# A seven-product form for five instead of four of the eight pairs of k-tiles in the gate and up products of a fused decoder kernel

## The chip, the cores and the metric

The kernel runs on one core of a Trainium2 chip. Time is the device time of the whole program in microseconds (us), the median of several runs. One more execution was profiled; its trace gives every instruction a start, a duration and, where its engine stood idle before it, the instruction that ended the idle time. Engines are called as in the profile: PE (TensorE, the matmuls), PEld (its weight loads), DVE (VectorE), ACT (ScalarE), POOL (GpSimd), SP (SyncE, which issues the loads).

## The reference, cut to what matters

The program is two residual blocks over 256 tokens of width 2048 in float32. The change touches only the last sublayer, the gated feed-forward layer with a hidden width of 5632:

```python
hf = rms_norm_2(x, g_ffn[layer])
x = x + (jax.nn.silu(hf @ w_gate[layer]) * (hf @ w_up[layer])) @ w_down[layer]
return rms_norm_2(x, g_final)
```

## The kernel before

**Split operands.** Each float32 operand is kept as a high part (a copy in the fp32r type, `hi`, `xh`, `wsh`) and a low part (the operand minus its high part, `lo`, `xl`, `wsl`). A product is three matmuls: high by high, high by low, low by high. For weights ACT makes the high part and DVE the low part, from a landed block `raw`. A block is 512 rows by 512 columns (1 MB); the copies work on halves of it (128 x 1024 elements), and `hi` and `lo` hold four halves each (HS = LS = 4), so ACT and DVE can be at most four halves ahead of PE. There are four `raw` blocks; SP loads a block again once DVE has made the last low part of the block that was in it.

**The feed-forward layer** runs in turns `i` of 512 hidden columns. Turns 0 and 1 are plain. In turns 2 to 10 (`ffn_turn`, nine of them) gate and up are computed together: step `v` (0 to 7) takes the pair of k-tiles 2v and 2v+1, and `raw` then holds four 128 x 512 parts, gate k0, gate k1 (half 0), up k0, up k1 (half 1), called w[0] to w[3] in the code. Two token halves times two k-tiles times gate and up are eight 128x128 by 128x512 products, 24 matmuls: a plain step (`plain_unit`). For the steps in the tuple `BILINEAR` it is a Strassen-Winograd scheme of seven products, 21 matmuls (`bilinear_unit`), on four sums of weight parts (`wsums`) and four of token parts (`sh`, `sl`, made once during turn 1 by `tokens_made`, `tokens_high`, `tokens_low`). The four weight sums are w0+w2, w2+w3, w0+w2+w3 and that plus w1. DVE makes them, ACT their high parts (`wsh`), DVE their low parts (`wsl`). Plain steps use differences of tokens, kept in `ah`/`al` and, for more than four plain steps, in `dh`/`dl`.

After step 7 follow four down-projection blocks of the turn before (units of 24 matmuls in `unit`). During them DVE adds up the seven products (`partial_sums`, `gate_sums`) and adds the down products to the residual X (`accumulate`, four a turn; the last, with c = 3, comes in step 1 of the next turn, where `hidden` and `hidden_blocks` also finish the hidden values of the turn before). Those go through DRAM and back, rearranged, into `fT` (POOL's queue), and `hidden_high` (ACT) and `hidden_low` (DVE) split them for the down blocks.

**Order.** Every engine runs its list in program order; nothing is reordered between engines but by semaphores. The wait of one instruction therefore holds back all that stands behind it on that engine. In a bilinear step DVE's list before is: two of the sums in one instruction (L2079, 1024 elements), low part of half 0, third sum (L2086), low parts of two sums (L2070), fourth sum (L2098), low part of w[3] alone (512 elements); the low parts of the other two sums stand in the next, plain step. ACT takes half 0, half 1 (only w[3], 512 elements), the first two sums (L1194), and the last two sums behind half 0 of the next step. The sums of the next turn's step 0 are made at the end of the down blocks (`start_next`). `gfb`, the gain row of the last norm (1 MB), is loaded in turn 0.

Of the kernel before, what the change touches and what calls it, by code (L numbers as in the profile page):

```python
# [52 lines left out]
BILINEAR = (0, 2, 4, 6)  # L53
# [72 lines left out]
def build(nc, x, ret_w_in, ret_w_out, pool_w_in, pool_w_grp, pool_b_grp, pool_w_out, final_norm, mem, positions,  # L126
# [3 lines left out]
    with ExitStack() as ctx:  # L130
# [6 lines left out]
        def stage(*tensors):  # L137
# [25 lines left out]
            ("sh", [P, len(BILINEAR), 4, P], F32R), ("sl", [P, len(BILINEAR), 4, P], F32R),  # L163
            ("dh", [P, max(0, KV - len(BILINEAR) - 4) + 1, SEQ], F32R), ("dl", [P, max(0, KV - len(BILINEAR) - 4) + 1, SEQ], F32R))
# [13 lines left out]
        junk = sb("junk", [P, NB])  # L178
        krT = sb("krT", [P, 2, SEQ])
        qrp = sb("qrp", [P, 2, TT, P])  # L180
# [46 lines left out]
        def as_blocks(tile):  # L227
# [44 lines left out]
        sg, fg, gfb, fblk, fT, wsums, wsh, wsl, p1s, u2 = stage(  # L272
            ("sg", [P, TT, NB]), ("fg", [P, TT, NB]), ("gfb", [P, D]),
            ("fblk", [P, TT, 4, 4 * BK]), ("fT", [P, TT * 4, 4 * BK]),
            ("wsums", [P, 4, NB]), ("wsh", [P, 4, NB], F32R), ("wsl", [P, 4, NB], F32R),
            ("p1s", [P, NB]), ("u2", [P, NB]))
        u3 = junk
# [39 lines left out]
        sums13_made, sum2_made, sum4_made = sem("sums13_made"), sem("sum2_made"), sem("sum4_made")  # L317
# [90 lines left out]
        def four(U):  # L408

            return raw[:, U % RAW].rearrange("p a b n -> p (a b) n")  # L410

# [57 lines left out]
        def _(sp):  # L469
# [166 lines left out]
            for u in range(4):  # L636
                load(Pos(FU + 2 * u), rows(w_gate[0], 512 * u, 0))
                load(Pos(FU + 2 * u + 1), rows(w_up[0], 512 * u, 0))
                if u == 1:
                    sp.wait_ge(half_used, 2 * FU)  # L640
                    sp.dma_start(gfb[:, :], g_final.rearrange("(a n) -> a n", a=1).broadcast_to([P, D])).then_inc(gf_in, 16)
# [10 lines left out]
            for j in range(4):  # L652
                load(Pos(DOWN_U + j), rows(w_down[0], (FC - 1) * NB, NB * j))
            out_v = out[0].rearrange("(t p) d -> p t d", p=P)
# [52 lines left out]
        def _(act):  # L707
# [441 lines left out]
            def tokens_high(v):  # L1149

                act.wait_ge(tok_made, v + 1)
                if v in BILINEAR:
                    dst, srcs = sh[:, BILINEAR.index(v)], x_sums
# [20 lines left out]
            def pair_high(U, i, v, h):  # L1174
# [6 lines left out]
                k = slice(1, 2) if h and v in BILINEAR else slice(0, 2)  # L1181
                act.activation(hi[:, (U.at * 2 + h) % HS, k, :], raw[:, U % RAW, h, k, :], ACT.Copy).then_inc(hi_ready, 1)  # L1182

            def high_sums(i, v, part):

                n = sums_at(i, v)
                if part == 0:
                    act.wait_ge(sums13_made, n + 1)
                else:
                    act.wait_ge(sum4_made, n + 1)  # L1190
                if n:
                    act.wait_ge(sums_used, 2 * n - 1 + part)
                at = slice(2 * part, 2 * part + 2)
                act.activation(wsh[:, at, :], wsums[:, at, :], ACT.Copy).then_inc(sums_high, 1)  # L1194
# [77 lines left out]
        def _(dve):  # L1272
# [708 lines left out]
            def tokens_made(v):  # L1981

                ks = slice(2 * v, 2 * v + 2)
# [10 lines left out]
            def tokens_low(v):  # L1994

                dve.wait_ge(tok_high, v + 1)
                if v in BILINEAR:
                    n = BILINEAR.index(v)
                    dst, high, srcs = sl[:, n], sh[:, n], x_sums
# [834 lines left out]
```

## Time and profile before

| | |
|---|---|
| median of 3 runs | 2486.75 us (2486.75 to 2487.12) |
| the profiled execution: its own time | 2486.79 us |
| its span, first to last instruction | 2485.0 us |
| PE busy, 10962 matmuls | 2472.1 us (99%) |
| DVE busy | 1771.4 us (71%) |
| ACT busy | 1276.0 us (51%) |
| granted TensorE clock, mean | 0.999 of full speed |

The profiled execution took 2486.79 us, 1.8 us more than its span, and agrees with the median of the timed runs. How to read it: durations of neighbouring instructions on one engine overlap in the trace by a little, so what an instruction costs in a row of others is the distance between starts. "Idle before" names the time in which the engine stood still and who ended it.

### The profile page before, as it was taken

What the parts mean: (1) busy time and instruction counts of PE and PEld (TensorE: products, weight loads), DVE (VectorE), ACT (ScalarE), POOL (GpSimd) and SP (SyncE); (2) the same over time, 40 slices, a digit from 0 to 9 for tenths busy, and PEclk for the clock granted to TensorE, in tenths of its full rate; (3) what the DMA queues carried; (4) which work ended last, traced back from release to release, by engine and by line L of the source; (5) the groups of instructions that cost most, each with busy time, mean ns of one, the idle gap of its engine ahead of it and who ended that gap; (6) DMA issues with size and microseconds to landing.
All of it is one profiled execution on the core that took longest, in us unless ns stands there. A gap on an engine that the chain in (4) does not pass through costs nothing.

```text
span 2485.0 us, 28892 instructions
## 1 busy us (share of the span) xinstructions
PE 2472.1 (99%) x10962; PEld 2036.7 (82%) x10962; DVE 1771.4 (71%) x2253; ACT 1276.0 (51%) x1619; POOL 192.0 (8%) x319
## 2 busy tenths in 40 slices
PE   9999999999999999999999999999999999999998
PEld 7888788888888888888888889888888888888887
DVE  6665665665675666675666866776678899988897
ACT  6454444444555444444545556566555555555554
POOL 0010000000011000010001100010100000000000
PEclk9999999999999999999999999999999999999999
DMA  9667666666688777776778754667766666666664
GB/s 333 208 223 221 208 212 211 204 218 202 210 241 259 231 233 223 226 234 210 228 238 262 235 180 149 233 203 220 229 211 220 220 217 212 210 211 218 218 210 148
DMA packets 263610, 545.31 MB, mean 219 GB/s; under 512 B 14768, under 2 KB 21040, under 8 KB 263088
## 3 DMA queue, kind: packets, MB, share of 16 engines
q1 hardware_dynamic: 242304, 477.39, 59.3%
q0 software_dynamic: 21168, 66.08, 9.5%
q8 instruction: 87, 1.43, 0.2%
q14 instruction: 51, 0.42, 0.1%
HBM read 508.29 MB, written 35.13 MB: 219 GB/s over the span
## 4 chain that ended last, share of the span: by engine, by line
PE 92%; DVE 5%; issue 2%; ACT 0%; DMA 0%; POOL 0%; DVEq 0%; ACTq 0%
PE job L2266 25%; PE job L2267 25%; PE job L2272 25%; DVE lo L2060 1%; PE group L2693 1%; PE group L2692 1%; PE group L2702 1%; PE att L2702 1%; PE att L2692 1%; PE att L2693 1%; PE job L2643 1%; PE job L2644 1%; PE job L2645 1%; DVE X L1343 1%; PE att L2643 1%
## 5 line engine op out<-in xcount | busy, mean ns | idle before, releaser
L1287 DVE TENSOR_TENSOR lo<-raw,hi 128x1024 fp32r<-128x1024 f32 (+1 forms) x736 | 879.2, 1213 | 504.8 <-ACT hi L729 483.9
L729 ACT ACTIVATE hi<-raw 128x1024 fp32r<-128x1024 f32 (+1 forms) x736 | 768.9, 1054 | 867.1 <-PE job L2272 808.9
L2266 PE MATMUL job<-hi,xh 128*128 128x512 f32 (+1 forms) x1696 | 663.0, 391 | 0.3 <-ACT hi L729 0.3
L2267 PE MATMUL job<-hi,xl 128*128 128x512 f32 (+1 forms) x1696 | 657.2, 388 | 0.0
L2272 PE MATMUL job<-lo,xh 128*128 128x512 f32 (+1 forms) x1696 | 451.0, 388 | 0.0
L2266 PEld LDWEIGHTS job<-hi,xh 128*128 128x128 f32 x1696 | 318.5, 188 | 68.5 <-issue 2.4
L2267 PEld LDWEIGHTS job<-hi,xl 128*128 128x128 f32 x1696 | 318.5, 188 | 66.4 <-issue 2.1
L2272 PEld LDWEIGHTS job<-lo,xh 128*128 128x128 f32 x1696 | 317.3, 188 | 65.1
L2266 PE MATMUL job<-hi,ah 128*128 128x512 f32 x832 | 325.9, 392 | 0.0
L2267 PE MATMUL job<-hi,al 128*128 128x512 f32 x832 | 323.8, 389 | 0.0
L2272 PE MATMUL job<-lo,ah 128*128 128x512 f32 x832 | 222.5, 389 | 0.0
L2266 PEld LDWEIGHTS job<-hi,ah 128*128 128x128 f32 x832 | 156.2, 188 | 32.8 <-issue 0.4
L2272 PEld LDWEIGHTS job<-lo,ah 128*128 128x128 f32 x832 | 156.2, 188 | 32.6
L2267 PEld LDWEIGHTS job<-hi,al 128*128 128x128 f32 x832 | 156.2, 188 | 32.3
L1182 ACT ACTIVATE hi<-raw 128x1024 fp32r<-128x1024 f32 (+1 forms) x144 | 133.2, 948 | 91.6 <-PE job L2272 42.8
L2060 DVE TENSOR_TENSOR lo<-raw,hi 128x1024 fp32r<-128x1024 f32 (+1 forms) x144 | 153.8, 1082 | 4.4 <-ACT hi L1182 4.4
L2266 PE MATMUL job<-hi,mh 128*128 128x512 f32 (+1 forms) x400 | 155.3, 388 | 0.2 <-ACT hi L729 0.2
L2267 PE MATMUL job<-hi,ml 128*128 128x512 f32 (+1 forms) x400 | 154.0, 385 | 0.0
L1343 DVE TENSOR_TENSOR X<-job,X 128x512 f32<-128x512 f32 x168 | 107.8, 683 | 63.2 <-PE job L2272 62.9
L1194 ACT ACTIVATE wsh<-wsums 128x1024 fp32r<-128x1024 f32 x72 | 76.1, 1057 | 75.8 <-DVE wsums L2079 59.8
L2272 PE MATMUL job<-lo,mh 128*128 128x512 f32 (+1 forms) x400 | 105.3, 385 | 0.0
L2070 DVE TENSOR_TENSOR wsl<-wsums,wsh 128x1024 fp32r<-128x1024 f32 x72 | 87.5, 1215 | 0.0
(409 smaller groups left out, 2534.5 us busy)
## 6 DMA issues: line engine op xcount, KB each, us to landing
raw<-in_ret_w_in SPq DMA_DIRECT2D x94, 1024.0 KB, 5.2
raw<-in_pool_w_in SPq DMA_DIRECT2D x64, 1024.0 KB, 5.6
raw<-in_w_down SPq DMA_DIRECT2D x44, 1024.0 KB, 5.2
raw<-in_w_gate SPq DMA_DIRECT2D x72, 512.0 KB, 3.9
raw<-in_w_up SPq DMA_DIRECT2D x72, 512.0 KB, 4.8
raw<-in_ret_w_out SPq DMA_DIRECT2D x32, 1024.0 KB, 5.3
raw<-in_pool_w_out SPq DMA_DIRECT2D x32, 1024.0 KB, 5.3
raw<-in_w_in SPq DMA_DIRECT2D x28, 1024.0 KB, 6.0
```

Source lines behind the costliest of these rows:

```text
L729: act.activation(hi[:, (U.at * 2 + h) % HS, :, 0:n], src, ACT.Copy).then_inc(hi_ready, 1)
L1182: act.activation(hi[:, (U.at * 2 + h) % HS, k, :], raw[:, U % RAW, h, k, :], ACT.Copy).then_inc(hi_ready, 1)
L1194: act.activation(wsh[:, at, :], wsums[:, at, :], ACT.Copy).then_inc(sums_high, 1)
L1287: dve.tensor_tensor(lo[:, (U.at * 2 + h) % LS, :, 0:n], src, hi[:, (U.at * 2 + h) % HS, :, 0:n].bitcast(F32), ALU.subtract).then_inc(lo_re ...
L1343: ins = dve.tensor_tensor(xs, pair[J % 2][t][:, :], xs, ALU.add)
L2060: dve.tensor_tensor(lo[:, (U.at * 2 + h) % LS, k, :], raw[:, U % RAW, h, k, :], hi[:, (U.at * 2 + h) % HS, k, :].bitcast(F32), ALU.subtrac ...
L2070: dve.tensor_tensor(wsl[:, at, :], wsums[:, at, :], wsh[:, at, :].bitcast(F32), ALU.subtract).then_inc(sums_low, 1)
L2266: pe.matmul(o, oh[:, kt, ts], w, start=first and k == 0, stop=False)
L2267: pe.matmul(o, ol[:, kt, ts], w, start=False, stop=False)
L2272: ins = pe.matmul(pair[J % 2][t][:, 0:n], oh[:, kt, ts], lo[:, H % LS, k, 0:n], start=False, stop=last and k == 1)
L2643: pe.matmul(o, oh, wh, start=start, stop=False)
L2692: pe.matmul(o[:, :], oh, hi[:, H, k], start=opens and k == 0, stop=False)
```

## The change

The tuple becomes `(0, 2, 3, 5, 6)`: step 3 and step 5 take the seven-product form and step 4 gives it up, which makes five such steps and three plain ones. With it:

- The sum w0+w2 is written in place over w[2] in `raw`; half 1 of the block then holds that sum and w[3], and is copied and subtracted as a full half. ACT's copy of half 1 waits for the sum (`sum1_made`).
- The other three sums stand in `wsums` (3 x 512) and go through ACT in one instruction and through DVE in one, of 1536 elements. `wsh` and `wsl` have two places used in turn.
- The four sums are four DVE instructions of 512 elements instead of one of 1024 and two of 512. The last two wait each for the one that it builds on.
- ACT's copy of the sums comes behind both halves of its own step and ahead of the next step's; DVE's low part of them comes at the head of the next step where that is bilinear (3 and 6), else behind the low part of its half 0 (1, 4 and 7).
- PE does four products (12 matmuls) of a bilinear step before it needs the sums, then three (9 matmuls).
- `hidden_high` and `hidden_low` move from step 6 to step 4.
- The fifth set of token sums lies over `krT` and another place, and turn 1 makes the tokens of step 6 last. The load of `gfb` moves behind the last weight load.

```diff
-BILINEAR = (0, 2, 4, 6)
+BILINEAR = (0, 2, 3, 5, 6)
...
             def pair_high(U, i, v, h):
...
                     act.wait_ge(up_landed[U % RAW], up_count(i, v))
+                    if v in BILINEAR:
+                        act.wait_ge(sum1_made, sums_at(i, v) + 1)
...
+            def high_sums(i, v):
 
                 n = sums_at(i, v)
+                act.wait_ge(sum4_made, n + 1)
+                if n >= 2:
+                    act.wait_ge(sums_used, n - 1)
+                act.activation(wsh[:, n % 2, :, :], wsums[:, :, :], ACT.Copy).then_inc(sums_high, 1)
...
                 for v in range(KV):
                     pair_high(U + v, i, v, 0)
-                    if v - 1 in BILINEAR:
-                        high_sums(i, v - 1, 1)
                     pair_high(U + v, i, v, 1)
                     if v in BILINEAR:
-                        high_sums(i, v, 0)
-                    if v == 6:
+                        high_sums(i, v)
+                    if v == 4:
                         hidden_high(I, ah)
...
+            def first_sums(U, i, v):
...
+                if n:
+                    dve.wait_ge(sums_low, n)
+                dve.tensor_tensor(wsums[:, 0, :], w[:, 3, :], w[:, 2, :], ALU.add)
+                dve.tensor_tensor(w[:, 2, :], w[:, 0, :], w[:, 2, :], ALU.add).then_inc(sum1_made, 1)
 
+            def last_sums(U, i, v):
 
                 n, w = sums_at(i, v), four(U)
+                dve.wait_ge(sum1_made, n + 1)
+                dve.tensor_tensor(wsums[:, 1, :], w[:, 2, :], w[:, 3, :], ALU.add).then_inc(sum2_made, 1)
+                dve.wait_ge(sum2_made, n + 1)
+                dve.tensor_tensor(wsums[:, 2, :], wsums[:, 1, :], w[:, 1, :], ALU.add).then_inc(sum4_made, 1)
 
             def bilinear_low(U, i, v):
...
                 if v:
+                    first_sums(U, i, v)
                 low_of(U, 0, slice(0, 2))
                 if v:
+                    last_sums(U, i, v)
+                low_of(U, 1, slice(0, 2))
...
                     if v in BILINEAR:
+                        if v - 1 in BILINEAR:
+                            low_sums(i, v - 1)
                         bilinear_low(U + v, i, v)
                     else:
                         low_of(U + v, 0, slice(0, 2))
                         if v == 1:
                             accumulate(J - 1, U, 3)
                         if v - 1 in BILINEAR:
-                            low_sums(i, v - 1, 1)
+                            low_sums(i, v - 1)
                         low_of(U + v, 1, slice(0, 2))
...
                 wait_pair(U, 1)
+                product(BANK5[:, :], s_high[:, 1], s_low[:, 1], hi[:, b, 0], lo[:, b, 0], opens, closes)
+                product(BANK3[:, :], s_high[:, 3], s_low[:, 3], hi[:, b, 1], lo[:, b, 1], opens, closes).then_inc(half_used, 1)
+                pe.wait_ge(sums_low, n + 1)
```

DVE's list in steps 2 and 3 of a turn, before (`wsums` are the sums, `wsl` their low parts; the first row is step 2's first):

```order
L2079 TENSOR_TENSOR wsums<-raw 128x1024
L2060 TENSOR_TENSOR lo<-raw,hi 128x1024
L2086 TENSOR_TENSOR wsums<-wsums,raw 128x512
L2070 TENSOR_TENSOR wsl<-wsums,wsh 128x1024
L2098 TENSOR_TENSOR wsums<-wsums,raw 128x512
L2060 TENSOR_TENSOR lo<-raw,hi 128x512
L2060 TENSOR_TENSOR lo<-raw,hi 128x1024
L2070 TENSOR_TENSOR wsl<-wsums,wsh 128x1024
L2060 TENSOR_TENSOR lo<-raw,hi 128x1024
```

The same stretch of the changed kernel (`raw<-raw` is the sum in place; the x2 near the end is half 1 of step 3 and half 0 of step 4):

```order
L2085 TENSOR_TENSOR wsums<-raw 128x512
L2086 TENSOR_TENSOR raw<-raw 128x512
L2067 TENSOR_TENSOR lo<-raw,hi 128x1024
L2092 TENSOR_TENSOR wsums<-raw 128x512
L2094 TENSOR_TENSOR wsums<-wsums,raw 128x512
L2067 TENSOR_TENSOR lo<-raw,hi 128x1024
L2076 TENSOR_TENSOR wsl<-wsums,wsh 128x1536
L2085 TENSOR_TENSOR wsums<-raw 128x512
L2086 TENSOR_TENSOR raw<-raw 128x512
L2067 TENSOR_TENSOR lo<-raw,hi 128x1024
L2092 TENSOR_TENSOR wsums<-raw 128x512
L2094 TENSOR_TENSOR wsums<-wsums,raw 128x512
```

Step 3 has become a second full set of sums, and the low part of step 2's sums now stands ahead of it in one piece.

ACT's list from step 2 to half 1 of step 5, before (`wsh` are the high parts of the sums):

```order
L1182 ACTIVATE hi<-raw 128x512
L1194 ACTIVATE wsh<-wsums 128x1024
L1182 ACTIVATE hi<-raw 128x1024
L1194 ACTIVATE wsh<-wsums 128x1024
L1182 ACTIVATE hi<-raw 128x1024 x2
L1182 ACTIVATE hi<-raw 128x512
L1194 ACTIVATE wsh<-wsums 128x1024
L1182 ACTIVATE hi<-raw 128x1024
L1194 ACTIVATE wsh<-wsums 128x1024
```

And of the changed kernel from step 0 to step 6 (the x4 are both halves of steps 1 and 2, then each x2 is one step):

```order
L1193 ACTIVATE hi<-raw 128x1024 x2
L1201 ACTIVATE wsh<-wsums 128x1536
L1193 ACTIVATE hi<-raw 128x1024 x4
L1201 ACTIVATE wsh<-wsums 128x1536
L1193 ACTIVATE hi<-raw 128x1024 x2
L1201 ACTIVATE wsh<-wsums 128x1536
L1193 ACTIVATE hi<-raw 128x1024 x2
L1181 ACTIVATE ah<-fT 128x1024
L1193 ACTIVATE hi<-raw 128x1024 x2
L1201 ACTIVATE wsh<-wsums 128x1536
L1193 ACTIVATE hi<-raw 128x1024 x2
L1201 ACTIVATE wsh<-wsums 128x1536
```

Before, one half of the next step went ahead of the last two sums; now both halves of the next step stand behind all three.

## Rows read from the trace of the kernel before

**Rows 1.** The page: busy time by engine and the chain that ended last.

```profile
PE 2472.1 (99%) x10962; PEld 2036.7 (82%) x10962; DVE 1771.4 (71%) x2253; ACT 1276.0 (51%) x1619; POOL 192.0 (8%) x319
...
PE 92%; DVE 5%; issue 2%; ACT 0%; DMA 0%; POOL 0%; DVEq 0%; ACTq 0%
```

**Rows 2.** Busy time by stretch: start:end, length, PE, PEld, DVE, ACT, POOL, clock, DMA.

```profile
2109.50:2173.10 63.60, 63.31 (x277) 51.63 (x277) 57.12 (x65) 33.91 (x36) 3.04 (x5) 1.00 0.66 214
```

**Rows 3.** Timeline of PE (start us, duration us, instruction): borders of turns.

```profile
2136.53 0.39 PE L2643 MATMUL job<-hi,xh 128*128 128x512 f32 x1
...
2138.57 0.40 PE L2643 MATMUL att<-wsh,sh 128*128 128x512 f32 x1
...
2141.38 0.39 PE L2692 MATMUL group<-hi,xh 128*128 128x512 f32 x1
...
2148.65 0.47 PE L2643 MATMUL att<-hi,sh 128*128 128x512 f32 x1 [0.29 <-DVE lo L2060]
...
2178.41 0.39 PE L2266 MATMUL job<-hi,ah 128*128 128x512 f32 x1
...
2200.17 0.39 PE L2643 MATMUL job<-hi,xh 128*128 128x512 f32 x1
```

**Rows 4.** Timeline of DVE over one turn, rows chosen; idle time in brackets.

```profile
2109.47 0.68 DVE L2105 TENSOR_TENSOR u<-job,p1s 128x512 f32<-128x512 f32 x1
2110.19 0.69 DVE L2106 TENSOR_TENSOR junk<-job,u 128x512 f32<-128x512 f32 x1
2113.41 1.23 DVE L1287 TENSOR_TENSOR lo<-raw,hi 128x1024 fp32r<-128x1024 f32 x1 [2.53 <-ACT hi L729]
2114.97 0.69 DVE L2112 TENSOR_TENSOR sg<-group,p1s 128x512 f32<-128x512 f32 x1 [0.34 <-PE att L2702]
...
2120.41 1.29 DVE L1343 TENSOR_TENSOR X<-job,X 128x512 f32<-128x512 f32 x2 [1.10 <-PE job L2272]
...
2125.85 1.29 DVE L1343 TENSOR_TENSOR X<-job,X 128x512 f32<-128x512 f32 x2 [1.89 <-PE job L2272]
...
2137.11 1.28 DVE L1343 TENSOR_TENSOR X<-job,X 128x512 f32<-128x512 f32 x2
2138.31 1.21 DVE L2070 TENSOR_TENSOR wsl<-wsums,wsh 128x1024 fp32r<-128x1024 f32 x1
...
2140.57 1.41 DVE L2035 SCALAR_TENSOR_TENSOR fg<-fg,stat,sg 128x512 f32<-128x512 f32 x2
...
2143.24 1.18 DVE L2079 TENSOR_TENSOR wsums<-raw 128x1024 f32<-128x1024 f32 x1
...
2147.22 0.68 DVE L2098 TENSOR_TENSOR wsums<-wsums,raw 128x512 f32<-128x512 f32 x1
2147.82 1.82 DVE L2060 TENSOR_TENSOR lo<-raw,hi 128x512 fp32r<-128x512 f32 x2
```

**Rows 5.** Timeline of ACT in step 2 of the same turn.

```profile
2147.93 1.06 ACT L1194 ACTIVATE wsh<-wsums 128x1024 fp32r<-128x1024 f32 x1 [1.46 <-DVE wsums L2098]
2148.90 2.51 ACT L1182 ACTIVATE hi<-raw 128x1024 fp32r<-128x1024 f32 x3
```

**Rows 6.** Groups by line and shape on ACT, 1884 to 2485 us: count, busy, mean ns.

```profile
L1194 ACT ACTIVATE wsh<-wsums 128x1024 fp32r<-128x1024 f32 x70 | 74.0, 1057 | 75.5 <-DVE wsums L2079 59.8 <-DVE wsums L2098 14.8
L1182 ACT ACTIVATE hi<-raw 128x512 fp32r<-128x512 f32 x35 | 21.7, 619 | 13.3 <-PE job L2272 13.3
```

**Rows 7.** Timeline of POOL, and the time that the loads of fT took to land.

```profile
2147.52 2.32 POOL L678 DMA_DIRECT2D fT<-across  x4 [3.19 <-DMA across<-fblk]
...
DMA to landing us min/median/max: 2.7/5.5/8.7
```

**Rows 8.** Busy time by stretch after the last matmul; the column behind POOL is the clock.

```profile
2478.00:2480.00 2.00, 0.00 (x0) 0.00 (x0) 1.47 (x6) 1.36 (x4) 0.00 (x0) 1.00 0.00 0
2480.00:2482.00 2.00, 0.00 (x0) 0.00 (x0) 0.69 (x2) 0.87 (x2) 0.00 (x0) 0.87 0.57 212
2482.00:2485.00 3.00, 0.00 (x0) 0.00 (x0) 0.00 (x0) 0.00 (x0) 0.00 (x0) 0.50 0.60 208
```

More of the change, by code:

```diff
@@ L271, in build @@
         x_blk[3] = xL[3][0].rearrange("p (t q) c -> p t q c", q=4)
[L272 to L275, printed above, removed]
+        sg, fg, fblk, fT, wsums, wsh, wsl, p1s, u2 = stage(
+            ("sg", [P, TT, NB]), ("fg", [P, TT, NB]),
+            ("fblk", [P, TT, 4, 4 * BK]), ("fT", [P, TT * 4, 4 * BK]), ("wsums", [P, 3, NB]),
+            ("wsh", [P, 2, 3, NB], F32R), ("wsl", [P, 2, 3, NB], F32R),
             ("p1s", [P, NB]), ("u2", [P, NB]))
+        _, gfb = stage(("ffn_front", [P, 11 * NB]), ("gfb", [P, D]))
         u3 = junk
@@ L410, in four, with combined @@
             return raw[:, U % RAW].rearrange("p a b n -> p (a b) n")
+        TOKENS = [v for v in range(KV) if v != BILINEAR[-1]] + [BILINEAR[-1]]
+        def combined(s, high):
+            if s < 4:
+                return (sh if high else sl)[:, s]
+            return (sh_last if high else sl_last)[:, :, :]
         def difference(v, high):
@@ L653, in _ @@
                 load(Pos(DOWN_U + j), rows(w_down[0], (FC - 1) * NB, NB * j))
+            sp.wait_ge(sums_used, NBIL * (FC - PAIRED))
+            sp.dma_start(gfb[:, :], g_final.rearrange("(a n) -> a n", a=1).broadcast_to([P, D])).then_inc(gf_in, 16)
             out_v = out[0].rearrange("(t p) d -> p t d", p=P)
@@ L1179, in pair_high @@
                     act.wait_ge(up_landed[U % RAW], up_count(i, v))
+                    if v in BILINEAR:
+                        act.wait_ge(sum1_made, sums_at(i, v) + 1)
                 act.wait_ge(half_used, U.value(2, h - HS + 1))
-                k = slice(1, 2) if h and v in BILINEAR else slice(0, 2)
-                act.activation(hi[:, (U.at * 2 + h) % HS, k, :], raw[:, U % RAW, h, k, :], ACT.Copy).then_inc(hi_ready, 1)
-            def high_sums(i, v, part):
+                act.activation(hi[:, (U.at * 2 + h) % HS, :, :], raw[:, U % RAW, h, :, :], ACT.Copy).then_inc(hi_ready, 1)
+            def high_sums(i, v):
                 n = sums_at(i, v)
[L1187 to L1194, printed above, removed]
+                act.wait_ge(sum4_made, n + 1)
+                if n >= 2:
+                    act.wait_ge(sums_used, n - 1)
+                act.activation(wsh[:, n % 2, :, :], wsums[:, :, :], ACT.Copy).then_inc(sums_high, 1)
             drain(Pos(FJ), Pos(FU + 7), lambda t: sg[:, t, :], RS, ACT.Silu)
@@ L2061, in low_of, with low_sums @@
                                   hi[:, (U.at * 2 + h) % HS, k, :].bitcast(F32), ALU.subtract).then_inc(lo_ready, 1)
[L2063 removed]
+            def low_sums(i, v):
                 n = sums_at(i, v)
[L2066 to L2072 removed]
+                dve.wait_ge(sums_high, n + 1)
+                if n >= 2:
+                    dve.wait_ge(sums_used, n - 1)
+                dve.tensor_tensor(wsl[:, n % 2, :, :], wsums[:, :, :], wsh[:, n % 2, :, :].bitcast(F32), ALU.subtract).then_inc(sums_low, 1)
+            def first_sums(U, i, v):
                 n, w = sums_at(i, v), four(U)
@@ L2167, in ffn_turn @@
                         hidden(i - 1)
[L2168 removed]
+                    if v == 4:
                         hidden_low(I, al, ah)
```

66 lines of the change are left out of this document (22 added, 44 removed).

## Prediction

> **What bounds the kernel now.** I read the page first: PE is busy for 99% of the span and makes up 92% of the chain that ended last, DVE 5% [rows 1]. The change touches only the nine turns from 2 to 10, so I took the table by stretch next. One turn takes 63.6 us; PE is busy for 63.3 of them and DVE for 57.1 [rows 2]. That is an engine with 6.5 us left, which is why the third view is the timeline of DVE: its idle time in a turn is 2.53 + 0.34 + 1.10 + 1.89 = 5.9 us, and all of it lies in the down blocks, where DVE waits for PE (directly, or through ACT, whose copy waits for PE) [rows 4]. Such idle time can't be used for work of steps 0 to 7. In those steps DVE has next to nothing left: from its last accumulate on it runs without a stop, and in step 2 PE waits 0.29 us for it [rows 3, 4]. So PE is the bound, by a hair, and only because its own work of steps 0 to 7 is about as long as that of DVE. In time the turn has two parts [rows 3]: steps 0 to 7, from 2136.53 to 2178.41, 41.9 us; four down blocks, to 2200.17, 21.76 us for 96 matmuls, 0.2267 each.
>
> **What PE saves.** A bilinear step has 21 matmuls and a plain one 24, so three fall away in each of nine turns: 27 x 0.2267 = 6.1 us. Matmuls on the sums cost a little more, (2141.38 - 2138.57) / 12 = 0.234 [rows 3]; there are nine a step of them now instead of twelve.
>
> **What DVE pays, by starts [rows 4].** 512 elements cost 0.60 us (2147.22 to 2147.82), 1024 cost 1.13 (2138.31 to 2140.57 for two). An instruction that waits for its own predecessor costs 0.72 instead of 0.60 (2109.47 to 2110.19). No row has 1536 elements. Bounds are 1.13 (as 1024) and 1.73 (1.13 + 0.60); from the slope 0.53 per 512 I take 1.67. For ACT the copy of 1024 takes 1.06 and of 512 0.62 [rows 6]; the one of 1536 is between 1.06 and 1.68, and by slope 1.50, its successor starting 0.09 before its end, as at 2147.93 and 2148.90 [rows 5]. The sum in place costs 0.60, as L2098, which also reads raw; below that it can't be, being the same 512 elements. A bilinear step costs DVE: before 1.13 + 0.60 + 0.60 for sums, 1.13 + 0.60 for low parts, 2 x 1.13 for low parts of sums, 6.3 in all; now 4 x 0.60 + 0.12, 2 x 1.13, 1.67, also about 6.4; a plain step 2 x 1.13 = 2.3. The fifth bilinear step thus adds 4.1, and the own waits 0.6, 4.7 us of DVE work a turn.
>
> **The new waits behind ACT.** ACT's copy of the sums stands ahead of both halves of the next step. Call s the start of DVE's last sum. It ends at s + 0.68; ACT starts 0.03 later (2147.22 + 0.68, then 2147.93 [rows 4, 5]), has the sums' high part at s + 2.21 and the next step's half 0 at s + 3.2. DVE needs 0.60 + 1.13 for the last sum and the low part of half 1 and is free at s + 1.73. Before a bilinear step (3, 6) it wants the sums first and stands 0.52 us; before a plain one (4, 7) it wants half 0 first and stands 1.51 us. Behind DVE's wait stands everything PE needs. That is 2 x 0.52 + 2 x 1.51 = 4.1 us a turn, which no row shows today: the nearest is 0.03 between the two engines, and the bounds are 0 (were ACT in time) and 4.7 (with the long ACT copy).
>
> **Laid end to end.** Let t = 0 be PE's start of step 0. DVE's accumulate starts at 0.20, the distance between PE's first down matmul and DVE's L2112 (2178.41 - 63.64 = 2114.77 against 2114.97 [rows 3, 4]). Now DVE has no gap but those waits: accumulate 1.20, low sums of step 0 1.67, half 1 of step 1 1.13, hidden 2.67 (2140.57 to 2143.24): 6.9. Steps 2, 3, 5 and 6 are each 0.60 + 0.60 + 1.13 + 0.60 + 0.12 + 0.60 + 1.13 = 4.8: 19.1. Low sums of 2, 3 and 5: 5.0. Half 0 of steps 4 and 7, half 1 of step 4, hidden_low: 4.5. The four waits: 4.1. That is 39.6; the low sums of step 6 take 1.75 more until they end, and PE starts 0.15 later (2147.82 + 0.68, then 2148.65 [rows 3, 4]): t = 41.5. From here PE runs on: 9 matmuls x 0.234 = 2.1, step 7 5.4, down blocks 21.8. The turn is **70.8 us instead of 63.6**. Without waits PE would reach the same point at 4 x (12 x 0.2267 + 9 x 0.234) + 2 x 5.44 + 2.7 = 32.9, so it stands 8.6 us a turn, in the largest pieces 2.95 us ahead of the sums of steps 3 and 6 (DVE there spends 1.51 + 1.13 + 1.67 on the path after half 1). In the down blocks DVE still waits for PE, as now, and does its 0.60 x 4 + 0.24 for the next step 0 under PE's matmuls: the queue there has 1.89 and 1.10 us of idle time to lose.
>
> **What costs nothing.** The hidden values move from step 6 to step 4. Their transposes end at about t = 6.9; before, POOL issued fT 4.3 us after that point, its last piece starts 1.74 us later and lands in 5.5 (at most 8.7) [rows 7]: 18.4, at worst 21.6. ACT comes to it at 21.0 and DVE wants the result at 24.1, so it fits even at worst; with that cover gone it would be at most 1 us a turn. The fifth token sum adds three small DVE instructions in turn 1: 0 to 1 us. The load of gfb now comes close to the last reload of fT: 0 as it stands behind the last weights in its queue, at most about 3 us once. Loads of weights get more time, not less.
>
> **The sum.** In turn 2 there is no hidden, 2.67 less on the DVE path: + 4.5. The eight others: 8 x 7.2 = 57.6. Together + 62 us on the profiled 2486.8 (the median of the runs is the same to 0.04 us): **2549 us**. The tail behind the last turn shifts and doesn't change.
>
> Here a rule can be set against a row. The row shows 0.12 us more where a DVE instruction waits for its predecessor [rows 4]. The Trainium skill ("VectorE: DVE Perf Modes", section "The DRAIN you can't avoid") says that a semaphore between such instructions costs nothing extra. By it the four own waits on the path would fall away, 4 x 0.12 x 9 = 4.3 us, and the sum would be 2545; the row decides.
>
> **The rivals.** A: PE stays the bound, and three matmuls less are what is seen: 2486.8 - 6.1 = **2480.7, faster**. For it speaks PE's 99% against DVE's 71% on the page [rows 1]; against it that 71% is an average over stages. Its place is the last sums of step 6, and it decides by one number: DVE would have to deliver them at t = 32.9 and not 41.5. 3%. The Trainium skill ("Perfetto Trace Analysis", section "Identifying the Most-Contended Engine") says to optimize the engine with the highest occupancy, but for TensorE to go by weight load busy time instead. The row of one turn has 51.6 us of PEld against 57.1 of DVE [rows 2], so read in that way it points away from A.
> B: ACT is in time and only DVE's work counts: 4.1 us a turn less, turn 66.7, 8 x 3.1 + 0.4 = + 25: **2512**. It would need ACT to copy out of order, or DVE to be late by other things anyway. 5%.
> C: TensorE's clock falls in PE's new pauses. At the end of the program the clock stayed at 1.00 for over 2 us after the last matmul and then went to 0.50, which is 1.2 GHz [rows 8]; the pauses here are 2.95 us at most, with dense matmuls between. If it stayed at that level for as long as a pause, PE would lose 1.5 us behind step 6 in each turn, where nothing covers it: + 13, **2562**; behind step 3 as well, 2576. 9%.
>
> **How the numbers follow.** The forecast has 83%. The range goes from 2530 (about half of the low bounds: sums of 1536 elements cheaper on DVE, up to 0.54 x 5 x 9 = 24 us, and on ACT, 0.44 x 4 x 9 = 16 us) to 2568 (the high ones, 2.7 + 6.5 us, the gfb load 3, and half of C). About 0.2%, 5 us, is what a measurement of this kernel can tell from no change. Faster by more than that is A, 3%; within it 2%, a DVE path far shorter than the rows say; slower 95%.
>
> **What would show it.** In the profile of the changed kernel: turns of 70.8 us; DVE idle for 0.5 us ahead of the low sums in steps 3 and 6 and for 1.5 us ahead of half 0 in steps 4 and 7, both ended by ACT; PE idle for about 3 us twice a turn ahead of its first matmul on `wsh`, ended by DVE's low sums; PE busy about 6 us less in sum; clock 1.00. I am wrong in the size if the 1536-element instruction isn't near 1.75 us, and in kind if DVE has idle time of its own in steps 2 to 6.

## The result: 2557 us, slower by 2.9%, and the profile after

| | before | after |
|---|---|---|
| median | 2486.75 us (2486.59 to 2487.12) | 2556.97 us (2556.4 to 2559.96) |
| ratio | | 1.0285, 95% interval 1.0267 to 1.0302 |
| span of the profiled execution | 2485.0 us | 2554.6 us |
| granted TensorE clock, mean | 0.999 | 0.993 |
| turn 2, then the ordinary turn | 62.96, 63.63 us | 68.57, 71.20 us |

The page of the profile after, busy time by engine and the chain that ended last, answers to [rows 1]:

```profile
PE 2491.2 (98%) x10935; PEld 2038.8 (80%) x10935; DVE 1816.4 (71%) x2301; ACT 1280.6 (50%) x1592; POOL 191.9 (8%) x319
...
PE 85%; DVE 9%; issue 3%; ACT 2%; DMA 0%; DVEq 0%; POOL 0%; ACTq 0%
```

The utilisation line (the first one) hardly moved: PE 98%, DVE 71%. What moved is the chain: DVE's part went from 5% to 9%, and ACT, which was at 0%, has 2%. The 27 matmuls are gone (10935 against 10962), yet PE's busy time rose by 19 us. "Busy" isn't work: a matmul next to a pause counts with its whole 0.39 or 0.50 us and not with the 0.2267 between starts. And some matmuls now run at half the clock: in the kernels of the experiments a turn in which that happens has 1.4 to 1.6 us more of PE busy time than one in which it doesn't, with the same matmuls.

The table by stretch (columns as in [rows 2]) of an ordinary turn, and of one of two that are longer:

```profile
2022.28:2093.48 71.20, 65.49 (x274) 51.93 (x273) 62.05 (x70) 34.44 (x33) 3.04 (x5) 0.98 0.59 192
2093.48:2166.26 72.78, 65.69 (x274) 51.85 (x273) 62.05 (x70) 34.44 (x33) 3.04 (x5) 0.98 0.59 188
```

DVE has 62.05 us of work in a turn instead of 57.12, and the turn is 71.20 instead of 63.60. The eight turn lengths after the first are 71.20, 71.20, 72.78, 71.57, 71.22, 71.20, 72.78, and the last, whose steps 0 to 7 take 49.45 us instead of 41.87. The tail from the start of the last turn's down blocks on takes 52.12 us against 52.05. So all of the difference lies in steps 0 to 7 of nine turns: 5.6 + 56.6 + 7.6 = 69.8 us, against 69.6 between the spans (turn 2 itself starts 0.2 us earlier than before).

Who made PE wait, from the view of waits of PE (total us, times, longest):

```profile
PE job L2649 <- DVE wsl L2076: 43.1, 35, 2.5
PE att L2649 <- DVE lo L2067: 7.4, 10, 0.9
PE job L2649 <- ACT hi L1193: 2.3, 8, 0.3
```

and who made DVE wait:

```profile
DVE lo L2067 <- ACT hi L1193: 24.6, 18, 1.4
DVE wsl L2076 <- ACT wsh L1201: 7.6, 18, 0.4
```

PE stands for the low parts of the sums, and DVE stands for ACT, both in the places that the prediction named: 18 waits of 1.4 us ahead of half 0 in steps 4 and 7, 18 of 0.4 us ahead of the low sums in steps 3 and 6. The profile puts no idle time of PE, ACT or DVE in the nine turns down to a load of weights. DVE's timeline from step 2 to the waits around it (start, duration; idle before in brackets) shows it row by row. The row at 2183.98 is the low part of half 1 of step 3, and the one at 2186.56 that of half 0 of step 4, with which the changed kernel's list goes on:

```profile
2174.30 1.22 DVE L2067 TENSOR_TENSOR lo<-raw,hi 128x1024 fp32r<-128x1024 f32 x1
2175.44 0.68 DVE L2092 TENSOR_TENSOR wsums<-raw 128x512 f32<-128x512 f32 x1
2176.16 0.69 DVE L2094 TENSOR_TENSOR wsums<-wsums,raw 128x512 f32<-128x512 f32 x1
2176.77 1.22 DVE L2067 TENSOR_TENSOR lo<-raw,hi 128x1024 fp32r<-128x1024 f32 x1
2178.41 1.76 DVE L2076 TENSOR_TENSOR wsl<-wsums,wsh 128x1536 fp32r<-128x1536 f32 x1 [0.42 <-ACT wsh L1201]
2180.30 0.69 DVE L2085 TENSOR_TENSOR wsums<-raw 128x512 f32<-128x512 f32 x1
...
2183.37 0.69 DVE L2094 TENSOR_TENSOR wsums<-wsums,raw 128x512 f32<-128x512 f32 x1
2183.98 1.22 DVE L2067 TENSOR_TENSOR lo<-raw,hi 128x1024 fp32r<-128x1024 f32 x1
2186.56 1.23 DVE L2067 TENSOR_TENSOR lo<-raw,hi 128x1024 fp32r<-128x1024 f32 x1 [1.36 <-ACT hi L1193]
2187.70 1.75 DVE L2076 TENSOR_TENSOR wsl<-wsums,wsh 128x1536 fp32r<-128x1536 f32 x1
2189.37 1.22 DVE L2067 TENSOR_TENSOR lo<-raw,hi 128x1024 fp32r<-128x1024 f32 x1
```

And ACT beside it, step 3's copies:

```profile
2184.09 1.49 ACT L1201 ACTIVATE wsh<-wsums 128x1536 fp32r<-128x1536 f32 x1 [1.35 <-DVE wsums L2094]
2185.48 1.99 ACT L1193 ACTIVATE hi<-raw 128x1024 fp32r<-128x1024 f32 x2
```

Read the last two fences together: ACT stands 1.35 us for DVE's last sum (2183.37, ready at 2184.06), copies the sums, and only then the half of step 4 that DVE waits for. The two engines wait for each other in turn.

### The profile page after: what moved, and what is told of

It reads as the page before. It is cut to its first block, busy times and chain, and to the rows that moved or that the text cites. A ratio compares the mean times of both kernels' runs of the same rounds, so it can differ in the third digit from the quotient of the medians.

```text
span 2554.6 us, 28840 instructions
## 1 busy us (share of the span) xinstructions
PE 2491.2 (98%) x10935; PEld 2038.8 (80%) x10935; DVE 1816.4 (71%) x2301; ACT 1280.6 (50%) x1592; POOL 191.9 (8%) x319
## 4 chain that ended last, share of the span: by engine, by line
PE 85%; DVE 9%; issue 3%; ACT 2%; DMA 0%; DVEq 0%; POOL 0%; ACTq 0%
PE job L2272 26%; PE job L2273 25%; PE job L2278 25%; DVE wsl L2076 2%; DVE lo L2067 2%; ACT wsh L1201 1%; DVE wsums L2094 1%; DVE raw L2086 1%; DVE wsums L2092 1%; ACT hi L1193 1%; PE group L2296 1%; DVE fg L2042 0%; DVE wsums L2085 0%; PE job L2649 0%; PE group L2699 0%
## 5 line engine op out<-in xcount | busy, mean ns | idle before, releaser
L1292 DVE TENSOR_TENSOR lo<-raw,hi 128x1024 fp32r<-128x1024 f32 (+1 forms) x736 | 879.4, 1213 | 497.6 <-ACT hi L738 486.4
L738 ACT ACTIVATE hi<-raw 128x1024 fp32r<-128x1024 f32 (+1 forms) x736 | 768.5, 1053 | 876.1 <-PE job L2278 807.0
L2278 PEld LDWEIGHTS job<-lo,xh 128*128 128x128 f32 x1696 | 317.3, 188 | 65.2
L1193 ACT ACTIVATE hi<-raw 128x1024 fp32r<-128x1024 f32 x144 | 150.0, 1054 | 173.2 <-DVE raw L2086 71.1
L2067 DVE TENSOR_TENSOR lo<-raw,hi 128x1024 fp32r<-128x1024 f32 x144 | 174.0, 1219 | 24.6 <-ACT hi L1193 24.6
L2273 PEld LDWEIGHTS job<-hi,al 128*128 128x128 f32 x832 | 156.2, 188 | 32.3
L1201 ACT ACTIVATE wsh<-wsums 128x1536 fp32r<-128x1536 f32 x45 | 66.9, 1486 | 48.6 <-DVE wsums L2094 48.6
L2272 PEld LDWEIGHTS job<-hi,mh 128*128 128x128 f32 x400 | 75.1, 188 | 14.6 <-issue 0.4
```

The source lines that it names most:

```text
L738: act.activation(hi[:, (U.at * 2 + h) % HS, :, 0:n], src, ACT.Copy).then_inc(hi_ready, 1)
L1193: act.activation(hi[:, (U.at * 2 + h) % HS, :, :], raw[:, U % RAW, h, :, :], ACT.Copy).then_inc(hi_ready, 1)
L1201: act.activation(wsh[:, n % 2, :, :], wsums[:, :, :], ACT.Copy).then_inc(sums_high, 1)
L1292: dve.tensor_tensor(lo[:, (U.at * 2 + h) % LS, :, 0:n], src, hi[:, (U.at * 2 + h) % HS, :, 0:n].bitcast(F32), ALU.subtract).then_inc(lo_re ...
L2067: dve.tensor_tensor(lo[:, (U.at * 2 + h) % LS, k, :], raw[:, U % RAW, h, k, :], hi[:, (U.at * 2 + h) % HS, k, :].bitcast(F32), ALU.subtrac ...
L2272: pe.matmul(o, oh[:, kt, ts], w, start=first and k == 0, stop=False)
```

## The experiments

All are edits of the changed kernel unless said otherwise. In every comparison the kernel before took 2486.8 or 2486.9 us. The theory was: DVE's list, lengthened by its waits for ACT, sets the turn. Its rivals: PE's own rate of matmuls, the new form as such, and the clock.

**Four steps in the new form.** Does the form cost something, or only the fifth step?

```diff
-BILINEAR = (0, 2, 3, 5, 6)
+BILINEAR = (0, 2, 4, 6)
```

> The new form of a step, but only four steps of seven products as before, (0, 2, 4, 6). Theory (DVE's list and its waits behind ACT set the turn): DVE has 0.6 us of own waits more than before and stands 1.4 us behind ACT in front of half 0 of steps 3, 5 and 7; laid end to end a turn takes 67.1 us where it was 63.6, so about 2515 us (2508 to 2522). Rival (the fifth step alone costs the time, the new form nothing): 2487 us, same as before. By how far it is above 2487 it tells what part of the 70 us belongs to the form and what to the fifth step.

Measured: 2518.47 us (2517.66 to 2518.87), 1.0127 times before, interval 1.0112 to 1.0143. The same 10962 matmuls as before, and 31.6 us more: almost half of the loss comes from the form and its order, without a fifth step. The waits of this kernel:

```profile
DVE lo L2067 <- ACT hi L1193: 24.6, 18, 1.4
...
PE job L2649 <- DVE wsl L2076: 24.4, 21, 2.3
...
DVE al L2058 <- ACT ah L1181: 12.3, 9, 1.4
```

DVE's waits of 1.4 us for ACT stand there too, and at three places a turn instead of two: ahead of half 0 in steps 3 and 7, and in step 4 ahead of the low part of the hidden values, which ACT splits behind its copy of the sums. The clock fell in this kernel as well, behind five of its PE pauses of 2.3 us, at 0.5 us a turn: turns with a fall take 67.5 to 67.6 us, the others 67.05 to 67.10. The fifth step adds 2556.97 - 2518.47 = 38.5 us.

**ACT's copy of the sums behind half 0 of the next step** instead of behind both halves of its own, as it was before.

```diff
                     pair_high(U + v, i, v, 0)
+                    if v - 1 in BILINEAR:
+                        high_sums(i, v - 1)
                     pair_high(U + v, i, v, 1)
-                    if v in BILINEAR:
-                        high_sums(i, v)
```

> The changed kernel, with ACT's copy of the sums moved behind half 0 of the next step; DVE's list is as it is. Theory: DVE's two waits of 1.4 us a turn in front of half 0 of steps 4 and 7 go, those of 0.4 us ahead of the sums of steps 2 and 5 stay; turns of 68.4 us instead of 71.2 to 72.8, 2557 - 9 x 2.8 = about 2532 us (2525 to 2536). Rival (DVE's work alone is the cause, its waits lie beside something else): 2557 us, no change.

Measured: 2530.98 us (2530.35 to 2532.07), 1.018 (1.0163 to 1.0197). That is in the expected range. Moving one instruction gives 26 us back, of which 3.2 are the two long turns: the clock never falls here. PE's waits for the low sums are as many as before but short:

```profile
PE job L2649 <- DVE wsl L2076: 24.1, 35, 1.1
```

**The same, and DVE takes half 0 ahead of the low sums in steps 3 and 6 too,** so that neither engine should stand for the other there.

```diff
             def bilinear_low(U, i, v):
-                if v:
+                if v - 1 in BILINEAR:
+                    low_of(U, 0, slice(0, 2))
+                    low_sums(i, v - 1)
                     first_sums(U, i, v)
-                low_of(U, 0, slice(0, 2))
+                else:
+                    if v:
+                        first_sums(U, i, v)
+                    low_of(U, 0, slice(0, 2))
...
                     if v in BILINEAR:
-                        if v - 1 in BILINEAR:
-                            low_sums(i, v - 1)
                         bilinear_low(U + v, i, v)
```

> As the one with ACT's order, and in steps 3 and 6 DVE makes the low part of half 0 ahead of the low parts of the sums of the step before. Theory: no DVE wait on ACT is left in steps 2 to 6; only DVE's work counts; turns of 67.4 us, about 2523 us (2515 to 2528), pauses of PE ahead of the sums under 2.2 us and so perhaps no fall of the clock any more. This is the rival B of the prediction run by itself. Rival (PE could be the bound then): 2481 us.

Measured: 2521.07 us (2520.57 to 2521.63), 1.0138 (1.0123 to 1.0153). This is rival B run by itself: five steps' work, and of the waits for ACT ahead of half 0 and of the low sums 0.6 us is left in all, in turn 2. One turn of it:

```profile
2084.22:2151.74 67.52, 63.80 (x274) 50.80 (x273) 61.87 (x70) 34.22 (x33) 3.05 (x5) 1.00 0.62 203
```

DVE's work is as in the change (61.87 against 62.05), the turn 67.52, the clock 1.00. So of 70.2 us the two orders make 35.9; what is left is 34.3. Not all of the 35.9 are waits: 3.2 are the clock, which no longer falls in the turns, and 0.4 one long wait that isn't there (see below).

**Eight matmuls a turn taken away** (the low-part product of half 0 in the plain steps 1 and 4, which leaves that term out of the result).

```diff
                             pe.matmul(o[:, :], oh, hi[:, H, k], start=opens and k == 0, stop=False)
-                            pe.matmul(o[:, :], ol, hi[:, H, k], start=False, stop=False)
+                            if h or v == 7:
+                                pe.matmul(o[:, :], ol, hi[:, H, k], start=False, stop=False)
```

> The changed kernel without the high by low matmuls of half 0 in the plain steps 1 and 4 of turns 2 to 10 (the gate's low token parts are left out there): 8 of 273 matmuls a turn less, 16.3 us of PE time in sum. Theory (DVE is the bound from the accumulate to the last sums): within 3 us of 2557 us. Rival (PE is the bound): 2541 us.

Measured: 2557.94 us (2557.28 to 2559.17), 1.0287 (1.0272 to 1.0302). 72 matmuls fewer bring nothing; at 0.2267 us they would be 16 us if PE were the bound. The 1 us more fits the clock: three turns of this kernel are long (72.6 us), not two. A turn:

```profile
2094.78:2165.99 71.21, 63.85 (x267) 50.32 (x265) 62.07 (x70) 34.43 (x33) 3.05 (x5) 0.98 0.59 192
```

PE's 1.6 us less of busy time became idle time. That is the plainest answer to "three matmuls less a turn": they were cut from an engine that had become the one that waits.

**DVE's work made short.** Both orders, and the four sums of every step but the very first (turn 2, step 0) made on 64 of 512 columns; the other columns keep old values, so the result isn't the reference's. The last two sums are cut in the same way.

```diff
+                c = slice(0, NB) if n == 0 else slice(0, 64)
-                dve.tensor_tensor(wsums[:, 0, :], w[:, 3, :], w[:, 2, :], ALU.add)
-                dve.tensor_tensor(w[:, 2, :], w[:, 0, :], w[:, 2, :], ALU.add).then_inc(sum1_made, 1)
+                dve.tensor_tensor(wsums[:, 0, c], w[:, 3, c], w[:, 2, c], ALU.add)
+                dve.tensor_tensor(w[:, 2, c], w[:, 0, c], w[:, 2, c], ALU.add).then_inc(sum1_made, 1)
```

> The kernel with both orders, and with the four weight sums of every step made on 64 of 512 columns only (but for the very first step): the other columns keep old values, so the output isn't the reference's. It takes 4 x 0.45 us of DVE work off each step and leaves all waits and all matmuls. Theory (rival A of the prediction comes true once DVE's path is as short as PE's): turns of 62.5 to 63.2 us, 2478 to 2483 us, PE's waits for the sums nearly gone. If something else than DVE's time holds the five steps back: clearly above 2487 us.

Measured: 2484.14 us (2482.7 to 2485.68), 0.9989 (0.9979 to 0.9998). A turn:

```profile
2008.78:2071.92 63.14, 62.81 (x274) 51.03 (x273) 53.28 (x69) 34.46 (x33) 3.04 (x5) 1.00 0.66 216
```

DVE has 53.3 us of work, 8.6 less than with full sums, and PE fills its turn to 0.3 us. So rival A's picture is right as soon as its condition holds. Even then the gain is 0.1% and the time not 2480.7 us (nor the 2478 to 2483 expected, missed by 1 us): two turns were 1.4 us longer, because the reload of fT was late for step 4, of which more below, and the ordinary turn is 63.1 and not 62.9.

**Four steps and both orders.** The cost of a fifth step without the waits for ACT.

> Four steps (0, 2, 4, 6) in the new form with both orders. Theory: no DVE wait on ACT in front of half 0 of a step is left; DVE's work on the path to the last sums gives turns of 64.5 us: about 2495 us (2490 to 2500). Together with the kernel of five steps and both orders it gives the price of the fifth step without waits: about 26 us. Rival (the new form with four is as good as the old once the waits are gone): 2487 us.

Measured: 2498.36 us (2497.35 to 2498.71), 1.0046 (1.0031 to 1.0061). The shortest of the eight turns after the first take 64.55 us, one takes 66.30, the others up to 65.2. The fifth step in this form costs 2521.07 - 2498.36 = 22.7 us, 2.5 a turn, where 26 were expected; and the form with its own waits still costs 11.6 us over before. A part of both numbers is something else. In this kernel the hidden values come back late for step 4:

```profile
ACT ah L1181 <- DMA fT<-across: 16.1, 8, 3.4
...
DVE al L2058 <- ACT ah L1181: 5.3, 7, 2.0
```

The turns over 64.55 us are those in which DVE stands for them, 3.5 us in sum, and in the kernel with five steps and both orders it never does. Without them the fifth step costs 26 us, as expected, and the form 8 over before.

**Four steps at 0, 3, 5 and 7, both orders:** step 7's sums are then finished in the down blocks, where DVE has idle time. (Step 7's low sums stand between the halves of the first down block, ACT's copy likewise, and `gate_sums` also waits until PE has used them.)

```diff
-BILINEAR = (0, 2, 3, 5, 6)
+BILINEAR = (0, 3, 5, 7)
...
                 U = U + KV
-                split_lo(U)
+                split_lo(U, halves=(0,))
+                low_sums(i, 7)
+                split_lo(U, halves=(1,))
```

> Four steps in the new form with both orders, at (0, 3, 5, 7) instead of (0, 2, 4, 6). Step 7's low parts of the sums fall into the down blocks, where DVE has idle time, and step 2, in front of which DVE is latest, is plain. Laid end to end a turn takes 63.4 us, PE being the bound again: about 2484 to 2487 us, 11 us less than the same form at (0, 2, 4, 6), 2498. Rival (the places of the four steps don't matter, only DVE's sum): 2498 us.

Measured: 2492.27 us (2490.52 to 2495.82), 1.0023 (1.0013 to 1.0034): a miss by 5 to 8 us. Seven turns took 63.43 to 63.44, two took 65.44 and 66.29. In those, ACT and behind it DVE stood for the hidden values in step 4. ACT, then DVE, in the shorter of the two:

```profile
2157.49 1.06 ACT L1181 ACTIVATE ah<-fT 128x1024 fp32r<-128x1024 f32 x1 [3.57 <-DMA fT<-across]
...
2158.59 1.23 DVE L2060 TENSOR_TENSOR al<-fT,ah 128x1024 fp32r<-128x1024 f32 x1 [3.08 <-ACT ah L1181]
```

**The same with the hidden values' split back in step 6,** where it was before the change.

```diff
-                    if v == 4:
+                    if v == 6:
                         hidden_high(I, ah)
...
-                    if v == 4:
+                    if v == 6:
                         hidden_low(I, al, ah)
```

> Steps 0, 3, 5 and 7 in the new form with both orders, as in the run before that used these steps (2492.3 us, seven turns of 63.44 us and two of 65.4 and 66.3), and the split of the hidden values put back from step 4 to step 6 on ACT and DVE. Theory: the two long turns came from a late round trip of fT, which step 4 meets and step 6 does not. Then all nine turns are 63.4 to 63.5 us and the time is 2492.3 - 2.0 - 2.9 = about 2487. ACT shows no idle time that a transfer of fT ended. Rival: something else made the two turns long (the waits on the sums, the loads of the weights): they stay and the time is 2491 to 2493.

Measured: 2487.71 us (2487.06 to 2488.69), 1.0003 (0.9994 to 1.0012). ACT shows no idle time in the turns that a reload of fT ended, and the nine turns are regular, 63.43 us each on the mean. (It is no faster than before although its turns are 0.2 us shorter: once, ahead of the last four down blocks, PE stands 1.5 us for the low part of the last hidden values.) So the move to step 4 is free in the change only because its turn is late anyway; where the turn is short it costs 4.6 us over the program. A turn, DVE with 57.68 us in it:

```profile
2136.46:2199.90 63.44, 63.11 (x277) 51.75 (x276) 57.68 (x65) 33.44 (x32) 3.04 (x5) 1.00 0.68 216
```

**The clock: one pause at a time.** The change has two long PE pauses a turn, ahead of the sums of steps 3 and 6: 2.5 us each, the second 1.5 where the clock fell behind the first. Two kernels move ACT's copy for one of them only. First at step 4, which leaves the long pause behind step 6:

```diff
                     pair_high(U + v, i, v, 0)
+                    if v == 4:
+                        high_sums(i, 3)
                     pair_high(U + v, i, v, 1)
-                    if v in BILINEAR:
+                    if v in BILINEAR and v != 3:
                         high_sums(i, v)
```

> The changed kernel with ACT's copy of the sums behind half 0 of the next step at one place only, from step 3 to step 4: DVE's wait of 1.36 us there goes, that in step 7 stays. With DVE's list alone: 9 x 1.36 = 12 us less, 2545 us. With the clock as well: PE's pause in step 3 becomes too short to make the clock fall there, so in all nine turns it falls behind the pause in step 6, where nothing covers the slow matmuls (1.58 us more a turn, as in two of the nine turns of the changed kernel): 2557 - 12 + 7 x 1.6 = about 2556 us.

Measured: 2552.29 us (2551.66 to 2553.03), 1.0263 (1.0248 to 1.0279). And the same edit at step 7 (`v == 7`, `high_sums(i, 6)`, `v != 6`), which leaves the pause behind step 3:

> The same at the other place only, from step 6 to step 7. With DVE's list alone: 2545 us. With the clock as well: it falls behind the pause in step 3 in all turns, under cover of DVE, and never behind step 6: 2557 - 12 - 2 x 1.6 = about 2542 us. The pair is what tells: with the clock this one is about 14 us faster than its twin, without it they are equal.

Measured: 2540.13 us (2539.78 to 2541.86), 1.0216 (1.02 to 1.0231). The edit is the same, the gain is 4.7 us in one place and 16.8 in the other: 12.2 between the two where 14 were expected, and 0 without the clock. But the clock did not fall behind every long pause, as had been expected. The stretches right behind the long pause, one with and one without a fallen clock, of the first kernel:

```profile
2062.00:2066.00 4.00, 3.84 (x10) 3.03 (x11) 4.00 (x5) 0.50 (x2) 0.00 (x0) 0.57 0.44 116
2419.00:2423.00 4.00, 3.90 (x17) 3.21 (x18) 4.00 (x5) 0.44 (x1) 0.00 (x0) 1.00 0.43 121
```

and of the second:

```profile
2112.00:2116.00 4.00, 3.70 (x9) 2.93 (x10) 4.00 (x6) 0.35 (x2) 0.00 (x0) 0.57 0.40 107
2182.00:2186.00 4.00, 3.97 (x17) 3.27 (x18) 4.00 (x5) 0.47 (x1) 0.00 (x0) 1.00 0.38 116
```

In the first kernel the clock fell behind step 6's pause in 7 of 9 turns, and those after turn 2 are 71.3 to 71.7 us long instead of 69.74. In the second it fell behind step 3's pause in 5 of 9, and the turns after turn 2 are 69.73 to 69.76 us either way (70.09 once). Behind step 3 a slower PE is covered: it would have waited for DVE at step 6 anyway. Behind step 6 nothing covers it, 1.58 us each time; 7 x 1.58 = 11.1 of the 12.2 us between the two.

**The kernel before, with the hidden values formed in step 3** instead of step 1. The one edit is to the kernel before: DVE does 2.67 us of `hidden` later, so the low parts for steps 1 and 2 come earlier.

```diff
-                    if v == 1 and i > PAIRED:
+                    if v == 3 and i > PAIRED:
                         hidden(i - 1)
```

> The kernel before, with one edit: DVE finishes the hidden values of the turn before (2.7 us) behind step 3 instead of step 1. If DVE's list is what holds PE by a hair in step 2 even before the change, PE's 0.29 us in front of that step's third product go, and the turn comes down from 63.64 towards 62.85 us (276 matmuls without a wait): 2480 to 2485 us. Rival (PE alone is the bound): 2487 us, no change. If the hidden values come back too late for ACT in step 6, slower.

Measured: 2482.1 us (2481.65 to 2483.35), 0.9981 (0.9972 to 0.999): faster than both kernels, by 0.2% against the kernel before. All turns take 62.96 us, PE without a gap:

```profile
2134.85:2197.81 62.96, 62.96 (x277) 51.83 (x276) 57.08 (x65) 34.02 (x37) 3.05 (x5) 1.00 0.66 217
```

DVE's work is the same 57.1 us. It was never too much for the turn; it stood in the wrong place. The price that was feared is there too, but covered: in eight turns ACT stands for the late hidden values in step 6, and behind it DVE in six, while PE never waits:

```profile
ACT ah L1171 <- DMA fT<-across: 19.4, 8, 3.2
...
DVE al L2051 <- ACT ah L1171: 4.8, 6, 1.3
```

## Why the prediction was right, and where it was off

**The bound (right).** "PE is the bound, by a hair" and DVE's idle time "can't be used for work of steps 0 to 7": in the changed kernel DVE keeps the idle times of [rows 4] in its down blocks, 1.10 and 1.88 us ahead of the accumulates, while PE waits. DVE waits for PE in the down blocks and PE for DVE in steps 0 to 7, within one turn, and the page's 71% says nothing of either. The run without eight matmuls shows that PE no longer sets the time; the last run, on the kernel before with `hidden` moved, shows that the place of DVE's work cost 0.67 us a turn even before the change.

**PE's saving (right as priced, worth nothing).** 6.1 us would be seen only under rival A. Taking 72 more matmuls away changed nothing. But "PE busy about 6 us less in sum" was wrong: it rose by 19, for the two reasons given with the page; and the clock was 0.98 in a turn and not the 1.00 that was named as a sign.

**DVE's prices (right).** The groups by line and shape, 1884 to 2555 us of the changed kernel (count, busy, mean ns):

```profile
L2076 DVE TENSOR_TENSOR wsl<-wsums,wsh 128x1536 fp32r<-128x1536 f32 x45 | 78.9, 1754 | 7.6 <-ACT wsh L1201 7.6
```

1.754 us long and 1.67 from start to start (2187.70 to 2189.37), as taken from the slope; ACT's copy takes 1.49 (2184.09), estimated 1.50. DVE's work grew by 4.93 us a turn, reckoned 4.7. The own wait of 0.72 instead of 0.60 is there again (2175.44 to 2176.16). By it the Trainium skill's rule that a semaphore between such instructions costs nothing extra ("VectorE: DVE Perf Modes", section "The DRAIN you can't avoid"; measured there on copies) doesn't hold here; the sum made by it (2545) is 4.3 us further from the 2557 measured than mine.

**A term that I left out.** `first_sums` waits until the low sums ahead of it are finished, since it writes over `wsums`. In steps 3 and 6 that is DVE's own instruction right ahead: 1.89 us from start to start (2178.41 to 2180.30) instead of 1.67. I had counted the own waits inside `last_sums` and not this one, though it stands in the diff. It is there in all 18 places. Twice a turn it is 0.44. Against it, the waits for ACT at half 0 were a little shorter than 1.51: the row has 1.36 idle, by starts 2186.56 - (2183.98 + 1.14) = 1.44. The other wait came as reckoned, 0.42 in the row and 2178.41 - 2176.77 - 1.14 = 0.50 by starts, against 0.52. Together + 0.3 a turn: PE starts on step 6's sums at t = 41.8 (2064.06 - 2022.28) instead of 41.5. From there it takes 29.4 instead of 29.3, because the matmul behind the pause costs 0.34 (2064.06 to 2064.40) and not 0.23. That makes 71.20 instead of 70.8, about 3 us in all. Once (2199.21 in the same trace) the same own wait was 0.37 longer, for which I have no reason. It isn't an accident of one execution: the same instruction shows the same wait in the same turn, 6, in four of the other kernels with five steps.

**The waits behind ACT (right).** 24.6 + 7.6 = 32.2 us of DVE idle time in nine turns, reckoned 4.1 x 9 = 36.5 by starts. Taking them away gave 35.9 us, of which 3.6 are the clock and the one long wait, so 32.3 for the waits. That is the mechanism, and its size to 4 us.

**Rival B (its reason right, its price low).** It was said to be 2512; run by itself it is 2521.07. Its turn is 67.52 and not 66.7, 8 x 0.8 = 6.6 us, of which 0.44 a turn is the term left out. Turn 2 is 2.7 us over before and not 0.4; there the missing `hidden` shortened the turn by 1.9 and not by 2.67. In the trace DVE, earlier in that turn than in the others, catches up with ACT at the head of step 3 and stands 0.40 and 0.15 us for it, which it does in no other turn; that is most of the 0.8.

**Rival C (true in part).** I gave it 9% as something that happens every turn or not at all. It fell once in each of the nine turns: seven times behind step 3, where DVE covers it, and twice behind step 6, where it costs, in the long turns (they start at 2093.48 and 2380.25), 1.58 us each, 3.2 us. The price of 1.5 was right. PE's timeline behind the pause of step 6 in one of them, spaces of 0.43 us where 0.23 is usual:

```profile
2135.26 0.50 PE L2649 MATMUL job<-wsh,sh_last 128*128 128x512 f32 x1 [2.55 <-DVE wsl L2076]
...
2136.36 0.63 PE L2649 MATMUL job<-wsh,sh_last 128*128 128x512 f32 x1
2136.79 0.63 PE L2650 MATMUL job<-wsh,sl_last 128*128 128x512 f32 x1
```

And in an ordinary turn, pauses of steps 3 and 6:

```profile
2045.53 0.50 PE L2649 MATMUL job<-wsh,sh 128*128 128x512 f32 x1 [2.53 <-DVE wsl L2076]
...
2064.06 0.50 PE L2649 MATMUL job<-wsh,sh_last 128*128 128x512 f32 x1 [1.54 <-DVE wsl L2076]
```

The second pause is a microsecond shorter there: PE, slowed behind step 3, came later to a point that DVE set. The prediction said 2.95 us at most; it is 2.55.

**Turn 2.** Reckoned + 4.5, measured 68.57 - 62.96 = 5.6. Before's turn 2 was shorter than the others by 0.67, which I hadn't looked at; with the term left out that is the 1.1 us.

**What costs nothing.** The load of `gfb`: right, the tail is equal to 0.1 us. The fifth token sum: right, turn 2 starts no later than before. The hidden values' split in step 4: right for this kernel, and for the stated reason, a cover (no idle time of ACT on fT in the turns of the change); without the cover I said "at most 1 us a turn", and the two bad turns cost 2.0 and 2.9 us. That bound was too low, but the mean over nine turns, 0.5, is inside it.

**The sum.** 2549 was 8 us short: 3 us the eight turns, of which most is the own wait, 3.2 the clock, 1.1 turn 2, 0.4 the one long wait, 0.5 the median over the profiled run.

**Rival A (its condition was the right one).** It needed the last sums of step 6 to be 8.6 us earlier. The run with short sums has 8.6 us less DVE work a turn than with full ones, and PE became the bound. That the two numbers are equal is chance: the sums of step 0 are made in the down blocks, so four fifths of the 8.6, 6.9 us, lie on the path, and 3.7 more a turn came from both orders. It isn't that DVE waits for ACT no more: it still stands 24.2 us in all for ACT's copies of halves. But that no longer holds PE back, which stands 4.8 us in all for the low sums, against 43.1 in the changed kernel. By the Trainium skill ("Perfetto Trace Analysis", section "Identifying the Most-Contended Engine") PE's weight load time was to be read in place of its occupancy; read so, DVE is the busier engine in the run with short sums (53.3 against 51.0 of PEld) and in the last run on the kernel before (57.1 against 51.8), and both are PE-bound, the second by order alone. Neither share told the bound; the idle rows of the stage did.

What stays open: why the clock fell behind one long pause and not behind the next, why the one own wait was longer in turn 6, and what the 8 us are made of that are left of the 11.6 of the form with four steps and both orders. Its own waits, 3 x 0.12 us and more a turn, explain a part. That the low sums in one piece come later than in two is a likely part too, but no run separates it.

## What to carry to other kernels

When two engines feed a third in lockstep, lay the step's list of each end to end, with the time at which each result is wanted, before removing work from the third; here a saving of 6 us on PE cost 70, half of it through where the copy of the sums on ACT and their low part on DVE stand. Idle time of an engine counts only in the stretch where the new work must stand: look at it by stage, and try a reordering first, since moving `hidden` by two steps (a digit in the code) brought 4.7 us where the rewrite lost 70. And ask of a step "moved at no cost" what cover it moved under, since it may lose it in the next version.

## What I had not expected of the hardware

- Clock: PE pauses of 1.5 to 2.55 us between dense matmuls, two a turn, were followed by a fall to 0.50 (1.2 GHz, the next 7 or 8 matmuls 0.43 us apart) in 9 of 18 cases in the changed kernel, once a turn. With the pauses taken one at a time it was 7 of 9 and 5 of 9, with eight matmuls fewer 12 of 18, and in the first kernel with four steps 5 of 8 (pauses of 2.3 us). In the turns of no kernel did it fall behind a pause of 1.9 us or less. Two pauses of the same length to 0.01 us can differ. A fall cost the turn 1.58 us where nothing covered it, 0.5 in the first kernel with four steps and nothing behind step 3, so its price must be given as a chance times what is uncovered, and not as a rule.
- Own waits on DVE cost more behind a long instruction: 0.12 us behind 512 elements (0.72 against 0.60 between starts), 0.22 behind 1536 (1.89 against 1.67).
- ACT takes a 1536-element copy in 1.49 us: three parts in one instruction cost 0.2 us less than 0.62 + 1.06. As a price the joining was no mistake. Whether it is one on the path isn't shown: the form with four steps and both orders is still 8 us over before.
